# Second attention loop of a two-block transformer kernel: order of scores, turns and values, three exponential buffers

## The reference

```
ya = chunk_mlp(p[..., :OFF_B], w_s, b_s)        # gated part: u * (w_s v + b_s)
q = apply_rope(_rms(p_q) * q_norm_w, cos, sin)  # 8 query heads of 64
k = apply_rope(_rms(k) * k_norm_w, cos, sin)    # 2 key heads; 256 keys + 256 of the context
yb = softmax(q k^T / 8) v                       # latent_attention, no mask
yc = hgrn_out(o, g, hgrn_norm_w)                # recurrent part: rms norm of o, times silu(g)
x = x + g1 * (concat(ya, yb, yc) @ w_out)
x = x + g2 * hier_moe(...)                      # 32 experts, top 2
```

## Time and profile before

| | |
|---|---|
| median of 3 runs | 1869.14 us (1865.86 to 1871.36) |
| the profiled execution, its own time | 1870.35 us |
| its span (first to last instruction) | 1868.2 us |
| PE busy | 1799.3 us, 96% |
| DVE, ACT, POOL busy | 871.7, 714.8, 146.5 us |
| mean granted TensorE clock | 0.984 of full |
| second block's attention loop, first turn to last copy | 1265.3 to 1320.8 us |
| output projection and router sums | to 1357 us |

### The profile page before, as it was taken

The page is one execution under the profiler, slowest core; times in us unless marked ns, Lnnn a source line. Parts: engine busy times, 40 slices in busy tenths (PEclk is TensorE's granted clock), DMA queues, the critical chain, the costliest instruction groups (busy, mean ns, idle before and its releaser), DMA issues.

```text
span 1868.2 us, 30528 instructions
## 1 busy us (share of the span) xinstructions
PE 1799.3 (96%) x12650; PEld 1463.1 (78%) x12650; DVE 871.7 (47%) x1530; ACT 714.8 (38%) x1187; POOL 146.5 (8%) x152
## 2 busy tenths in 40 slices
PE   7999999999999999999999999996879999999997
PEld 7999988999999999988999996783744444445443
DVE  6655666676557655665686663734120101011011
ACT  6444544454345434544464453533121112121111
POOL 1000132110001000132140000002000000000000
PEclk9999999999999999999999999996989999999999
DMA  9545564554554554464565552310549999999993
GB/s 381 174 168 180 162 218 165 192 186 166 178 176 164 179 179 162 157 231 176 194 221 181 181 184 76 82 66 1 226 161 409 426 422 427 428 424 427 421 430 135
DMA packets 75634, 425.71 MB, mean 228 GB/s; under 512 B 16000, under 2 KB 33664, under 8 KB 41728
## 3 DMA queue, kind: packets, MB, share of 16 engines
q1 hardware_dynamic: 75376, 421.53, 59.4%
q10 hardware_dynamic: 144, 2.56, 0.3%
HBM read 423.02 MB, written 1.05 MB: 227 GB/s over the span
## 4 chain that ended last, share of the span: by engine, by line
PE 87%; ACT 3%; DVE 3%; issue 3%; POOL 1%; POOLq 1%; DVEq 1%; DMA 0%; ACTq 0%; SPq 0%
PE ps L576 16%; PE ps L578 16%; PE ps L577 16%; PE ps L1194 12%; PE ps L1221 6%; PE ps L1174 3%; PE ps L1166 3%; PE ps L895 2%; PE ps L907 2%; PE ps L1142 2%; ACT w_split L1255 1%; PE ps L901 1%; PE ps L665 1%; DVE w_split L1644 1%; PE ps L748 1%
## 5 line engine op out<-in xcount | busy, mean ns | idle before, releaser
L1644 DVE TENSOR_TENSOR w_split<-ring,w_split 128x1024 fp32r<-128x1024 f32 x336 | 422.4, 1263 | 358.8 <-ACT w_split L1255 357.7
L576 PE MATMUL ps<-x_hi,w_split 128*128 128x272 f32 (+1 forms) x1856 | 541.8, 292 | 13.4 <-DVE w_split L1644 12.8
L578 PE MATMUL ps<-x_hi,w_split 128*128 128x272 f32 (+1 forms) x1856 | 534.8, 288 | 0.0
L577 PE MATMUL ps<-x_lo,w_split 128*128 128x272 f32 (+1 forms) x1856 | 532.8, 287 | 0.0
L1255 ACT ACTIVATE w_split<-ring 128x1024 fp32r<-128x1024 f32 x336 | 351.7, 1054 | 360.7 <-PE ps L578 360.0
L576 PEld LDWEIGHTS ps<-x_hi,w_split 128*128 128x128 f32 x1856 | 350.5, 189 | 24.0 <-issue 21.2
L577 PEld LDWEIGHTS ps<-x_lo,w_split 128*128 128x128 f32 x1856 | 350.4, 189 | 0.3
L578 PEld LDWEIGHTS ps<-x_hi,w_split 128*128 128x128 f32 x1856 | 350.3, 189 | 0.0
L1194 PE MATMUL ps<-ring,arena 128*64 128x512 f32 x1024 | 226.0, 594 | 1.7 <-issue 1.7
L576 PE MATMUL ps<-hid_hi,w_split 128*128 128x272 f32 (+1 forms) x704 | 201.6, 286 | 3.8 <-DVE arena L1731 3.8
L578 PE MATMUL ps<-hid_hi,w_split 128*128 128x272 f32 (+1 forms) x704 | 201.6, 286 | 0.0
(11 more groups left out here) (374 smaller groups left out, 1983.1 us busy)
## 6 DMA issues: line engine op xcount, KB each, us to landing
ring<-stream_expert SPq DMA_DIRECT2D x96, 2048.0 KB, 12.5
ring<-stream_ffn SPq DMA_DIRECT2D x131, 1024.0 KB, 4.9
ring<-stream_in SPq DMA_DIRECT2D x27, 1024.0 KB, 5.0
ring<-stream_mod SPq DMA_DIRECT2D x24, 1024.0 KB, 7.0
ring<-stream_out SPq DMA_DIRECT2D x12, 1024.0 KB, 5.0
ring<-stream_in SPq DMA_DIRECT2D x42, 256.0 KB, 3.9
con<-tables ACTq DMA_DIRECT2D x1, 2497.0 KB, 12.6
arena<-h_first SPq DMA_DIRECT2D x2, 544.0 KB, 4.5
```

The costliest lines, as they stand in the source:

```text
L576: pe.matmul(to, w[:, 0, k], hi, start=first, stop=False)
L577: pe.matmul(to, w[:, 0, k], lo, start=False, stop=False)
L578: return pe.matmul(to, w[:, 1, k], hi, start=False, stop=last_)
L1644: nc.vector.tensor_tensor(w[:, 1], half_of(n), w[:, 0].bitcast(fp32), ALU.subtract).then_inc(split_ready, 1)
```

## The change

- PE, ahead of the loop: behind projection q01 come the gated part's mixing, the head sums of the recurrent output (bank 4), projection q23 (bank 5), scores of pairs 0 and 1 (they need only q01, rotated), the sums of q, and all four groups of av (bank 6).
- PE, in the loop: `scores2(p + 2)` is issued ahead of `turn2(p)`, and `values2(p - 1)` behind it as before. The second half of the queries (q23) is waited for at pair 4.
- Exponentials and their statistics have three buffers (`AHEAD`); the third lies in the ring at `lev`. exp2(p) waits for turns p-3.
- ACT: av is copied out behind exponentials 0 and 1; in the loop the exponentials of p+2 come ahead of the copies of turned weights p.
- DVE: the gated part and the recurrent norm are done behind the rotation of q01, ahead of the maxima. `max2` is cut in two (`max2`, `shift2`), so that maxima 0 and 1 come ahead of the factors; q23 is rotated behind them. In the loop: max2(p+2), shift2(p+2), weights2(p+1), mixed2(p-2).
- POOL does the same work from the new buffers. No DMA is moved, added or removed.

```diff
+AHEAD = 3
...
-        ae = cut(arena, at_z, 2, 2, KEYS)
+        ae_of = [cut(arena, at_z, 2, KEYS), cut(arena, at_z + 2 * KEYS, 2, KEYS), lev[:, 0].rearrange("p (h s) -> p h s", h=2)]
...
-            pe.wait_ge(o2_sq_ready, 1)
-            pe.matmul(ps[:, 5, 0:512], half_ones, oh_sq, start=True, stop=True).then_inc(heads_summed, 1)
-            w = raw_slot(("in2", "q23"), 2, C, P)
-            evicted2("v")
-            queries(w, 2, 0)
-            queries(w, 2, 1).then_inc(proj_ready, 1)
-            w = raw_slot(("in2", "av"), C, P)
-            evicted2("u")
-            tokens(w, 0, 0, P, 0)
-            tokens(w, 0, P, P, 1)
-            evicted2("q23")
-            for i in range(2):
-                for j in range(4):
-                    at = 8 * i + 2 * j
-                    last = pe.matmul(ps[:, 4, at:at + 2], q_sq[:, j, i * P:i * P + P], half_ones[:, 0::64], start=True, stop=True)
-            last.then_inc(heads_summed, 1)
-            tokens(w, 0, 2 * P, P, 2)
-            tokens(w, 0, 3 * P, P, 3).then_inc(proj_ready, 1)
-
             pe.wait_ge(second_loaded, 48)
             pe.wait_ge(v_normed, 1)
+            pe.wait_ge(o2_sq_ready, 1)
...
             last.then_inc(mlp_mixed, 1)
-
-
-            pe.wait_ge(rotated, 3)
+            pe.matmul(ps[:, 4, 0:512], half_ones, oh_sq, start=True, stop=True).then_inc(heads_summed, 1)
+            w = raw_slot(("in2", "q23"), 2, C, P)
+            queries(w, 5, 0)
+            queries(w, 5, 1).then_inc(proj_ready, 1)
...
@@ -1071,9 +1055,12 @@
                 if p >= 2:
                     pe.wait_ge(s2_exp_ready, p - 1)
                 elif p == 0:
-                    evicted2("av")
+                    pe.wait_ge(rotated, 2)
+                    evicted2("q01")
                 else:
                     pe.wait_ge(heads_std_ready, K_STD)
+                if p == 4:
+                    pe.wait_ge(rotated, 3)
...
                 if p == 0:
                     pe.wait_ge(rq_ready, 1)
-                    pe.wait_ge(heads_std_ready, O_STD)
+                    evicted2("q23")
...
-                if p >= 1:
-                    pe.wait_ge(y2_ready, 2 + p - 1)
+                if p == 0:
+                    evicted2("av")
+                else:
+                    pe.wait_ge(y2_ready, 2 + max(p - 1, 0))
...
             scores2(0)
             scores2(1)
+            evicted2("q23")
+            pe.wait_ge(heads_std_ready, O_STD)
+            for i in range(2):
+                for j in range(4):
+                    at = 8 * i + 2 * j
+                    last = pe.matmul(ps[:, 4, at:at + 2], q_sq[:, j, i * P:i * P + P], half_ones[:, 0::64], start=True, stop=True)
+            last.then_inc(heads_summed, 1)
+            w = raw_slot(("in2", "av"), C, P)
+            for t in range(4):
+                last = tokens(w, 6, t * P, P, t)
+            last.then_inc(proj_ready, 1)
             for p in range(N_PAIRS):
-                turn2(p)
                 if p + 2 < N_PAIRS:
                     scores2(p + 2)
+                turn2(p)
                 if p >= 1:
                     values2(p - 1)
             values2(N_PAIRS - 1)
...
-            tile_done("av")
-            nc.scalar.activation(flat(av), ps[:, 0, 0:512], ACT.Copy).then_inc(proj2_evac, 1)
-
             def exp2(p):
 
                 a, b, i = pair_of(p)
                 act.wait_ge(s2_max_ready, p + 1)
-                if p >= 2:
-                    act.wait_ge(p2_turned, p - 1)
-                k = p % 2
+                if p >= AHEAD:
+                    act.wait_ge(p2_turned, p - AHEAD + 1)
+                k = p % AHEAD
                 for hh, head in enumerate((a, b)):
                     at = factor_at(head, i)
-                    last = nc.scalar.activation(ae[:, k, hh], ps[:, 2 * k + hh, 0:KEYS], ACT.Exp, bias=a_nmax[:, k, hh:hh + 1],
+                    last = nc.scalar.activation(ae_of[k][:, hh], ps[:, 2 * (p % 2) + hh, 0:KEYS], ACT.Exp, bias=a_nmax[:, k, hh:hh + 1],
                                                 scale=rqs[:, at:at + 1], accum_out=a_sum[:, k, hh:hh + 1])
                 last.then_inc(s2_exp_ready, 1)
 
             exp2(0)
             exp2(1)
+            tile_done("av")
+            nc.scalar.activation(flat(av), ps[:, 6, 0:512], ACT.Copy).then_inc(proj2_evac, 1)
             for p in range(N_PAIRS):
+                if p + 2 < N_PAIRS:
+                    exp2(p + 2)
                 act.wait_ge(p2_turned, p + 1)
                 if p >= 2:
                     act.wait_ge(pv2_ready, p - 1)
                 for hh in range(2):
                     last = nc.scalar.activation(aeT_of[p % 2][:, hh].rearrange("p t q -> p (t q)"), ps[:, 4 + hh, 0:512], ACT.Copy)
                 last.then_inc(p2T_ready, 1)
-                if p + 2 < N_PAIRS:
-                    exp2(p + 2)
...
-            for n, name in enumerate(("q01", "q23")):
+
+            def rotate2(n, name):
+
                 two = slice(2 * n, 2 * n + 2)
                 dve.wait_ge(proj2_evac, TILE2[name])
                 swapped(q_sin[:, two], aq[:, two], sin2, 2)
                 dve.wait_ge(cos_ready, n + 2)
                 nc.vector.tensor_tensor(aq[:, two], q_cos[:, two], q_sin[:, two], ALU.add).then_inc(rotated, 1)
-            dve.wait_ge(heads_std_ready, Q_STD)
-            nc.vector.reciprocal(q_std, q_std)
-            dve.drain()
-            nc.vector.tensor_scalar(rqs, q_std, 0.125, None, ALU.mult)
-            nc.vector.tensor_scalar(nrq, q_std, -0.125, None, ALU.mult).then_inc(rq_ready, 1)
-            dve.drain()
+
+            rotate2(0, "q01")
+            dve.wait_ge(mlp_mixed, 1)
+            nc.vector.tensor_tensor(mlp_mix, ps[:, 7, 0:512].rearrange("p (a b c) -> p a b c", a=2, b=2),
+                                    V("b_s", 2, P).unsqueeze(2).to_broadcast([P, 2, 2, P]), ALU.add)
+            dve.drain()
+            nc.vector.tensor_tensor(flat(y2[:, 0:2]), flat(mlp_u), mlp_mix.rearrange("p a b c -> p (a b c)"), ALU.mult).then_inc(y2_ready, 1)
+            dve.wait_ge(heads_std_ready, O_STD)
+            nc.vector.reciprocal(oh_std, oh_std)
+            dve.drain()
+            nc.vector.scalar_tensor_tensor(flat(oh), flat(oh), V("hgn"), oh_std, ALU.mult, ALU.mult)
+            dve.drain()
+            nc.vector.tensor_tensor(y2[:, 6:8], oh, hg, ALU.mult).then_inc(y2_ready, 1)
 
             def max2(p):
 
                 dve.wait_ge(s2_ready, p + 1)
-                k = p % 2
-                nc.vector.tensor_reduce(a_max[:, k], ps[:, 2 * k:2 * k + 2, 0:KEYS], AX.X, ALU.max)
+                nc.vector.tensor_reduce(a_max[:, p % AHEAD], ps[:, 2 * (p % 2):2 * (p % 2) + 2, 0:KEYS], AX.X, ALU.max)
                 dve.drain()
+
+            def shift2(p):
+
+                k = p % AHEAD
                 nc.vector.tensor_tensor(a_nmax[:, k], a_max[:, k], pair_factors(nrq, p), ALU.mult).then_inc(s2_max_ready, 1)
 
...
                 nc.vector.reciprocal(a_rsum[:, k], a_sum[:, k]).then_inc(rsum_ready, 1)
                 dve.drain()
-                nc.vector.tensor_scalar(ae[:, k, 0], ae[:, k, 0], a_rsum[:, k, 0:1], None, ALU.mult).then_inc(p2_ready, 1)
+                nc.vector.tensor_scalar(ae_of[k][:, 0], ae_of[k][:, 0], a_rsum[:, k, 0:1], None, ALU.mult).then_inc(p2_ready, 1)
...
             max2(0)
             max2(1)
+            dve.wait_ge(heads_std_ready, Q_STD)
+            nc.vector.reciprocal(q_std, q_std)
+            dve.drain()
+            nc.vector.tensor_scalar(rqs, q_std, 0.125, None, ALU.mult)
+            nc.vector.tensor_scalar(nrq, q_std, -0.125, None, ALU.mult).then_inc(rq_ready, 1)
+            dve.drain()
+            shift2(0)
+            shift2(1)
+            rotate2(1, "q23")
+            weights2(0)
             for p in range(N_PAIRS):
-                weights2(p)
-                if p == 0:
-                    dve.wait_ge(heads_std_ready, O_STD)
-                    nc.vector.reciprocal(oh_std, oh_std)
-                    dve.drain()
-                    nc.vector.scalar_tensor_tensor(flat(oh), flat(oh), V("hgn"), oh_std, ALU.mult, ALU.mult)
-                    dve.drain()
-                    nc.vector.tensor_tensor(y2[:, 6:8], oh, hg, ALU.mult).then_inc(y2_ready, 1)
-                if p == 1:
-                    dve.wait_ge(mlp_mixed, 1)
-                    nc.vector.tensor_tensor(mlp_mix, ps[:, 7, 0:512].rearrange("p (a b c) -> p a b c", a=2, b=2),
-                                            V("b_s", 2, P).unsqueeze(2).to_broadcast([P, 2, 2, P]), ALU.add)
-                    dve.drain()
-                    nc.vector.tensor_tensor(flat(y2[:, 0:2]), flat(mlp_u), mlp_mix.rearrange("p a b c -> p (a b c)"), ALU.mult).then_inc(y2_ready, 1)
                 if p + 2 < N_PAIRS:
                     max2(p + 2)
-                if p >= 1:
-                    mixed2(p - 1)
+                    shift2(p + 2)
+                if p + 1 < N_PAIRS:
+                    weights2(p + 1)
+                if p >= 2:
```

(19 more changed lines are left out.)

## The result

The changed kernel takes 1841.09 us (median of 4 runs, 1840.47 to 1842.46) against 1869.76 for the kernel before in the same comparison: a ratio of 0.9853 with a 95% interval of 0.9841 to 0.9865, which is 25 to 30 us less. Forecast were 1842.5 and 26.6 us less. The profiled execution took 1842.46 us with a span of 1840.4, 27.8 less than the span before.

The account below looks back on a forecast made before the run. PE's waits and half clock in the attention loop bound the kernel. The full-clock sum saves 27.9 us, less 1.3 for one half-clock stretch: 26.6 off the 1869.14 median gives 1842.5 us, range 1838.5 to 1853.

Parts of the forecast that it names:

- What bounds the kernel: Attention loop, 55.5 us: PE waits in queues and runs at mean clock 0.66; time saved there is saved at the end.
- (1) The stretch ahead: Ahead of the loop: reordered work stays 26.8 us without a gap; the hole from 1262.1 to 1265.3 goes.
- The thin slack: Ahead of the loop: q23's eviction on ACT ends 0.6 us before the sums of q; if gone, some tenths lost.
- (2) The cycle: In the loop at full clock: 7.68 us for two pairs, 3.84 a pair in place of 7.0.
- (3) The sum: From av's end at 1262.1 through cycles and tail at full clock: end 1292.9 against 1320.83, 27.9 us less.
- The clock: In the loop: full clock holds except one half-clock stretch behind pair 1's 2.1 us hole, costing 1.3 us.
- Rival A: Half clock throughout the loop, PE the bound at 6.15 us a pair: 12.5 us saved, 1856.6; chance 0.08.
- Rival B: Loop clock alternates as before, halfway between 3.84 and 6.15 us a pair: 20.2 us saved, 1848.9; chance 0.23.
- D: Half clock through the loop and on into the output projection: 23.7 us slower, 1892.8; chance 0.02.
- C: Loop turns still wait for POOL or ACT, period 6.5 us or more: under 5 us saved; chance 0.05.

Follow-up runs that it names:

- prologue_only: The changed kernel with the attention loop's old order and two exponential buffers, keeping the new order ahead of the loop: 1863.91 us against 1869.43 before the change.
- loop_only: The kernel before with the change's loop orders and three buffers, the old order kept ahead of the loop: 1850.47 us against 1869.43.
- before_dve_order: The kernel before with only DVE's reciprocal for pair p+1 moved behind the maximum of p+2, ahead of the copy-out of p-1: 1859.32 us against 1869.43.
- turns_first: The change with ACT's copies ahead of exponentials and pair 1's reciprocal early, but PE's turns ahead of scores as in the old loop: 1848.26 us.
- before_filled: The kernel before with two matmuls of constants added per pair, mostly in PE's idle time, no queue reordered: 1855.32 us against 1869.43.

## Why the prediction was right

*What bounds the kernel.* Right: of the 27.8 us of span 27.5 are there when the output projection begins (1293.33 in place of 1320.83), and the projection behind it kept its length. The medians differ by 28.7, 2.1 more than forecast; the rest of this part says where the sum was long.

*(1) The stretch ahead.* Right. PE has no gap from 1235.09 to the end of scores 3 at 1265.4. The thin slack, eviction of q23 against the sums of q, was there: the eviction ends at 1252.5 and the sums start at 1253.1, where I had the same two figures. `prologue_only` gives this part 5.5 us by itself.

*(2) The cycle.* The mechanism was right, turns wait for ACT's copy and not for POOL. The size was a little off: 7.38 us for two pairs where I had 7.68. The term mis-sized is the turns: two rows of 0.63 make 1.26, but eight turns in a row take 1.03 from start to start (1276.34 to 1277.37), since the row is 1.10 long and the next starts before it ends. That is 0.23 of the 0.30; the values, 1.02 from start to start where I had 1.09, are the rest. I called the third buffer free of cost and it is; it brings 2.2 us by the medians, 1.4 by the loop.

*(3) The sum.* From scores 2 to the output projection I had 30.8 us at full clock (1262.1 to 1292.9) and 32.1 with one stretch; the two profiles have 29.53 and 31.11. The sum was 1.3 long at full clock, 0.6 in the two cycles and the rest in the tail; with the stretch it was 1.0 long, because the stretch cost more than I gave it.

*The clock.* The single half-clock stretch behind the hole at pair 1 came in the first profile as forecast, cost 1.6 us where I had 1.3, and did not come in the second. PE did 1.28 us of work in the 3.40 around the hole and the clock fell; it did 3.30 in a stretch of the cycle and the clock stayed (the lines above). In the second profile PE did the same 1.28 in the 3.40 around the hole (1265.80 to 1269.20) and the clock stayed, so what these rows show does not tell the two apart; that the first profile met the forecast of exactly one stretch is in part luck. Rival A falls: nothing ran at half clock for long, and the loop with its sixteen sets of transposes ran at 1.00 when the hole did not break it. By the rule of the Trainium skill (TensorE: Matmul & The Clock Gate, Part 4) transposes do not count as activity; a third of PE's work in this loop would then be missing, and the clock of 1.00 shows no sign of it. Rival B falls with it: 0.95 and 1.00, not a half-and-half. Its argument had misread: the row that held has 1.08 us idle in 3.41, so a loop with 0.5 to 1 us idle a pair is busier than that row and does not lie between it and those that fell. And against D, that busy stretches had always led to a rise, holds for the rows it names; in `loop_only` PE worked 5.82 us without a gap at half clock. C and D did not come: POOL starts at 1273.8, 1277.1, 1281.2 and 1284.5 for pairs 3 to 6, every 3.3 to 4.1 us, and the output projection keeps 36.2 us at 1.00.

What the forecast did not say is how the gain is shared: about 9.7 us, a third, were to be had in the loop of the kernel before by the clock alone, for idle matmuls, and 10.1 by DVE's order alone, which raised the clock too. No run has the new orders at the old clock, so a clean split into waits and clock is not shown.

## What to carry to other kernels

Write down, for each engine, what stands behind the instruction that everybody waits for; a loop over engines is as long as its longest ring, and a ring closes through a queue's order as well as through data (`before_dve_order` and `turns_first` both stopped at 5.28 us a pair for this reason). When a loop waits on small steps, price the clock apart from the waits: idle-time matmuls on the old kernel do it in one run. Read their effect in the loop and not in the total: here 5.1 us of a profile's gain lay far from the place that was changed. After a reordering, ask again which copy the bound engine now waits for; here moving ACT's copies back in front gave 3 us more.

## What the runs showed of the hardware

The granted clock held at 2.4 GHz for 19.5 us with PE busy for 61% of it, with idle times of 1.3 and 0.6 us in each 5.3 (`before_dve_order`); in one part of it PE did only 1.48 us of work in 3.40:

```profile
1277.70:1281.10 3.40, 1.48 (x10) 1.11 (x12) 1.46 (x6) 1.79 (x5) 1.83 (x1) 1.00 0.00 0
```

In the kernel before, 1.33 in 3.40 was followed by 1.2 GHz. The same hole of 2.1 us in the same kernel was followed by 3.4 us at 1.2 GHz in one execution and by none in another, at 1.6 us of difference. PE's last matmuls behind the experts start 4.99 to 5.40 us after the ones before them in thirteen profiles and 1.99 in one (`before_filled`); no run shows the cause.
